# A transformer pair in one kernel: spill count read and Sqrt's table asked for before a stage barrier, second sum of squares of the first later layer taken from unscaled rows

## What is computed

```python
def rms_norm(x, w):
    xf = x.astype(jnp.float32)
    y = xf * lax.rsqrt(jnp.mean(xf * xf, axis=-1, keepdims=True) + NORM_EPS)
    return (y * w.astype(jnp.float32)).astype(x.dtype)
...
    return rms_norm(h, norm_final_w)          # end of the first block
...
    for l in range(DEPTH_2):
        h = rmsnorm(x, g_pre_mix[l])          # entry of a later layer
        y = token_mixer(h, w_in[l], ...)
        x = x + rmsnorm(y, g_post_mix[l])
        h = rmsnorm(x, g_pre_ffn[l])
        y = conv_ffn(h, w_up[l], ...)
        x = x + rmsnorm(y, g_post_ffn[l])
```

## Time and profile before

| what | value |
|---|---|
| median of 3 runs | 2921.39 us (2921.37 to 2924.36) |
| the profiled execution's own time | 2923.01 us |
| its span | 2921.1 us |
| mean granted TensorE clock, share of full | 0.97 |
| busy: PE, DVE, ACT, POOL | 2684.8, 1318.0, 873.6, 707.5 us |
| last unite on DVE | 1676.02 to 1677.24 |
| first Square of the entry | 1680.52 |
| first transposes of layer 0 | 1686.72 |
| first product of layer 0 | 1689.55 |

### The profile page before, as it was taken

The page is one execution under the profiler, slowest core; times in us unless marked ns, Lnnn a source line. Parts: engine busy times, 40 slices in busy tenths (PEclk is TensorE's granted clock), DMA queues, the critical chain, the costliest instruction groups (busy, mean ns, idle before and its releaser), DMA issues.

```text
span 2921.1 us, 35506 instructions
## 1 busy us (share of the span) xinstructions
PE 2684.8 (92%) x14188; PEld 1915.6 (66%) x14188; DVE 1318.0 (45%) x2403; ACT 873.6 (30%) x1643; POOL 707.5 (24%) x310
## 2 busy tenths in 40 slices
PE   8999999999988888888888789999999999899998
PEld 7997877888533333333333277688888776788887
DVE  4333745314633333333333367454444574644433
ACT  3333333423111111111111143543332344433332
POOL 4232233442000000000000122234445122344443
PEclk9999999999999999999999989999999999999999
DMA  3222211335999999999999721022232221122231
GB/s 142 87 88 103 78 65 37 107 114 210 382 427 427 429 428 429 428 429 429 428 429 428 332 85 58 30 87 87 93 109 87 90 89 58 58 87 87 89 113 72
DMA packets 126801, 572.19 MB, mean 196 GB/s; under 512 B 10705, under 2 KB 58193, under 8 KB 101329
## 3 DMA queue, kind: packets, MB, share of 16 engines
q1 hardware_dynamic: 121424, 561.08, 48.2%
q10 hardware_dynamic: 5248, 9.32, 1.0%
HBM read 566.12 MB, written 4.26 MB: 195 GB/s over the span
## 4 chain that ended last, share of the span: by engine, by line
PE 63%; DMA 25%; DVE 6%; ACT 3%; issue 1%; POOL 1%; POOLq 0%; SPq 0%; ACTq 0%; DVEq 0%
PE ps L342 39%; DMA wide<-in_moe_w 17%; PE ps L1262 8%; DMA arena<-in_moe_w 6%; PE ps L1690 4%; PE ps L1674 3%; PE ps L567 2%; PE ps L1060 1%; PE ps L538 1%; ACT ring_r L299 1%; PE ps L553 1%; DMA ring<-in_w_in 1%; DMA ring<-in_w_up 1%; PE ps L2604 1%; PE ps L2612 1%
## 5 line engine op out<-in xcount | busy, mean ns | idle before, releaser
L311 POOL TENSOR_TENSOR ring_r<-ring,ring_r 128x1024 fp32r<-128x1024 f32 (+2 forms) x284 | 692.5, 2471 | 2134.9 <-ACT ring_r L299 2134.9
L342 PE MATMUL ps<-xnT_r,ring_r 128*128 128x512 f32 (+1 forms) x1664 | 490.9, 378 | 9.9 <-DVE xn_r L2574 8.5
L342 PE MATMUL ps<-ring_r,xnT_r 128*128 128x512 f32 (+1 forms) x1360 | 446.3, 400 | 10.5 <-POOLq L255 5.0
L342 PEld LDWEIGHTS ps<-xnT_r,ring_r 128*128 128x128 f32 x1664 | 308.8, 191 | 69.8 <-DVE xn_r L2574 9.3
L342 PE MATMUL ps<-ring_r,arena_r 128*128 128x512 f32 x1392 | 329.9, 395 | 0.0
L342 PEld LDWEIGHTS ps<-ring_r,xnT_r 128*128 128x128 f32 x1360 | 290.0, 225 | 55.9 <-issue 11.6
L342 PE MATMUL ps<-xn_r,ring_r 128*128 128x512 f32 (+1 forms) x832 | 313.0, 376 | 0.0
L342 PEld LDWEIGHTS ps<-ring_r,arena_r 128*128 128x128 f32 x1392 | 262.3, 190 | 60.2 <-issue 5.4
L299 ACT ACTIVATE ring_r<-ring 128x1024 fp32r<-128x1024 f32 (+2 forms) x284 | 270.6, 1024 | 88.6 <-DMA ring<-in_w_down 68.3
L1674 PE MATMUL ps<-wide,arena 128*32 128x512 f32 x1536 | 199.3, 641 | 101.6 <-DMA wide<-in_moe_w 101.1
L1674 PEld LDWEIGHTS ps<-wide,arena 128*32 128x32 f32 x1536 | 42.0, 112 | 238.6 <-DMA wide<-in_moe_w 144.8
(11 more groups left out here) (358 smaller groups left out, 3681.1 us busy)
## 6 DMA issues: line engine op xcount, KB each, us to landing
wide<-in_moe_w SPq DMA_DIRECT2D x144, 2048.0 KB, 27.6
arena<-in_moe_w SPq DMA_DIRECT2D x48, 2048.0 KB, 27.4
ring<-in_w_in SPq DMA_DIRECT2D x25, 2048.0 KB, 8.1
ring<-in_w_up SPq DMA_DIRECT2D x22, 2048.0 KB, 8.5
ring<-in_w_down SPq DMA_DIRECT2D x10, 2048.0 KB, 7.8
ring<-in_w_out SPq DMA_DIRECT2D x6, 2048.0 KB, 8.1
ring<-in_w_ret_branch SPq DMA_DIRECT2D x2, 2048.0 KB, 8.7
attn_spill<-arena ACTq DMA_DIRECT2D x2, 1056.0 KB, 6.8
```

Source lines behind the costliest of these rows:

```text
L311: nc.gpsimd.tensor_tensor(ring_r[:, q % 2, cols], ring[:, q % 2, cols], ring_r[:, 2 + q % 2, cols].bitcast(F32), ALU.subtract).then_inc(ha ...
L342: ins = nc.tensor.matmul(bank, left, right, start=(start and k == 0), stop=(stop and k == 2))
```

## The change

Four things are changed, and only for the entry of the first later layer (`current["l"] == 0`) and the spill stage ahead of it.

The number of spills is read by `spill_count` ahead of the barrier on PE, DVE and ACT and handed to the spill functions; SP reads it where it did. ACT's small Sqrt for layer 0 stands between that read and the barrier, no longer at the entry.

DVE writes `xn` = `h` * `rows[:, 3]` for all four tiles (`gains_ready`). The branch of tile i then is the reciprocal, with `tile_added` on it, and h = xn * rstd, a tensor_scalar. Branches 0 and 1 stand in the loop behind products 0 and 1, products 2 and 3 behind them, and following 0 behind the loop.

Root h on ACT takes the Square of `xn` with rstd as its scale, and waits only for the reciprocal. The order of the roots in layer 0 becomes y0, h0, y1, h1, then behind the copies of tile 0 y2 and h2, behind those of tile 1 y3, behind those of tile 2 h3.

```diff
-        def spills(eng, body):
-            n = eng.value_load(spill_info[0:1, SPILL:SPILL + 1], min_val=0, max_val=SPILL)
+        def spill_count(eng):
+            return eng.value_load(spill_info[0:1, SPILL:SPILL + 1], min_val=0, max_val=SPILL)
+
+        def spills(eng, body, n):
             with eng.If(n > 0):
...
-                    for root in ((("h", 1), ("y", 3)), (("h", 2),), (("h", 3),), ())[k]:
+                    for root in enter_roots()[(4, 6, 7, 8)[k]:(6, 7, 8, 8)[k]]:
                         enter_root_act(a, *root)
...
+        FIRST_ENTER_ROOTS = [(what, i) for i in range(NT) for what in ("y", "h")]
         ENTER_ROOTS = [("y", 0), ("y", 1), ("h", 0), ("y", 2), ("h", 1), ("y", 3), ("h", 2), ("h", 3)]
...
-            if what == "h":
+            scale = 1.0
+            if what == "h" and current["l"] == 0:
+                a.wait_ge(Z.tile_added, i + 1)
+                x, scale = xn[:, i, :], small[:, BRANCH + 8 + i:BRANCH + 9 + i]
+            elif what == "h":
                 a.wait_ge(Z.tile_added, i + 1)
                 x = h[:, i, :]
...
-            nc.scalar.activation(Y.enter_squares[:, n % 2], x, ACT.Square, accum_out=small[:, base + i:base + i + 1]).then_inc(Z.sums_ready, 1)
+            nc.scalar.activation(Y.enter_squares[:, n % 2], x, ACT.Square, scale=scale, accum_out=small[:, base + i:base + i + 1]).then_inc(Z.sums_ready, 1)
...
             if current["l"]:
                 high_act(a, 0)
-            nc.scalar.activation(small[:, 30:31], table("eps"), ACT.Sqrt)
-            enter_root_act(a, "y", 0)
-            enter_root_act(a, "y", 1)
-            enter_root_act(a, "h", 0)
-            enter_root_act(a, "y", 2)
+                nc.scalar.activation(small[:, 30:31], table("eps"), ACT.Sqrt)
+            for root in enter_roots()[0:4]:
+                enter_root_act(a, *root)
...
-            link(nc.vector.reciprocal(rstd, small[:, BRANCH + 4 + i:BRANCH + 5 + i]))
+            ins = nc.vector.reciprocal(rstd, small[:, BRANCH + 4 + i:BRANCH + 5 + i])
             if current["l"] == 0:
-                nc.vector.scalar_tensor_tensor(out=h[:, i, :], in0=h[:, i, :], scalar=rstd, in1=rows[:, 3], op0=ALU.mult, op1=ALU.mult).then_inc(Z.tile_added, 1)
+                ins.then_inc(Z.tile_added, 1)
+                v.wait_ge(Z.tile_added, i + 1)
+                nc.vector.tensor_scalar(h[:, i, :], xn[:, i, :], rstd, None, ALU.mult).then_inc(Z.rows_normed, 1)
...
+                if current["l"] == 0:
+                    v.wait_ge(Z.rows_normed, i + 1)
                 rstd = small[:, NEXT + 8 + i:NEXT + 9 + i]
...
-            enter_branch_dve(v, link, 0)
-            enter_branch_dve(v, link, 1)
+            if current["l"] == 0:
+                for i in range(NT):
+                    nc.vector.tensor_tensor(xn[:, i, :], h[:, i, :], rows[:, 3], ALU.mult).then_inc(Z.gains_ready, 1)
+                    if i < 2:
+                        v.wait_ge(Z.gains_ready, i + 1)
+                        enter_branch_dve(v, link, i)
+                v.wait_ge(Z.gains_ready, NT)
+            else:
+                enter_branch_dve(v, link, 0)
+                enter_branch_dve(v, link, 1)
             v.wait_ge(pre_row_loaded, current["l"] * 16 + 16)
             following(0)
...
             experts_act(a)
+            spilled_n = spill_count(a)
+            nc.scalar.activation(small[:, 30:31], table("eps"), ACT.Sqrt)
             nxt()
-            spill_act(a)
+            spill_act(a, spilled_n)
```

More of the change, by code:

```diff
@@ L1936, in body, with spill_pe @@
                 sp.sem_inc(spill_next, 1)
-            spills(sp, body)
-        def spill_pe(pe):
+            spills(sp, body, spill_count(sp))
+        def spill_pe(pe, spilled_n):
             def body(j):
@@ L1964, in body, with spill_dve @@
                 pe.drain().then_inc(spill_used, 1)
-            spills(pe, body)
-        def spill_dve(v):
+            spills(pe, body, spilled_n)
+        def spill_dve(v, spilled_n):
             nc.vector.tensor_scalar(E.ahead, E.slot, -float(CAP * EXPERTS), None, ALU.add).then_inc(Z.shifted, 1)
@@ L1996, in body, with spill_act @@
                     unite_dve(i).then_inc(Z.tile_united, 1)
-            spills(v, body)
+            spills(v, body, spilled_n)
             v.drain().then_inc(Z.spills_united, 1)
-        def spill_act(a):
+        def spill_act(a, spilled_n):
             def body(j):
@@ L2009, in body @@
                 keep_y_act(0).then_inc(Z.y_act, 1)
-            spills(a, body)
+            spills(a, body, spilled_n)
         U_LAYERS = U_EXPERTS
@@ L2952, in down_banks, with enter_roots @@
             return ps[:, 2 * i:2 * i + 2, :].rearrange("p b n -> p (b n)")
+        def enter_roots():
+            return FIRST_ENTER_ROOTS if current["l"] == 0 else ENTER_ROOTS
         def enter_root_act(a, what, i, last=False):
             base = BRANCH if what == "y" else NEXT
-            n = i if last else ENTER_ROOTS.index((what, i))
-            if what == "h":
+            n = i if last else enter_roots().index((what, i))
+            scale = 1.0
[3 more added lines that the diff above has]
+            elif what == "h":
                 a.wait_ge(Z.tile_added, i + 1)
@@ L2987, in enter_branch_dve @@
         def enter_branch_dve(v, link, i, last=False):
-            v.wait_ge(Z.roots_ready, (i if last else ENTER_ROOTS.index(("y", i))) + 1)
+            v.wait_ge(Z.roots_ready, (i if last else enter_roots().index(("y", i))) + 1)
             rstd = small[:, BRANCH + 8 + i:BRANCH + 9 + i]
-            link(nc.vector.reciprocal(rstd, small[:, BRANCH + 4 + i:BRANCH + 5 + i]))
+            ins = nc.vector.reciprocal(rstd, small[:, BRANCH + 4 + i:BRANCH + 5 + i])
             if current["l"] == 0:
-                nc.vector.scalar_tensor_tensor(out=h[:, i, :], in0=h[:, i, :], scalar=rstd, in1=rows[:, 3], op0=ALU.mult, op1=ALU.mult).then_inc(Z.tile_added, 1)
+                ins.then_inc(Z.tile_added, 1)
+                v.wait_ge(Z.tile_added, i + 1)
+                nc.vector.tensor_scalar(h[:, i, :], xn[:, i, :], rstd, None, ALU.mult).then_inc(Z.rows_normed, 1)
             else:
+                link(ins)
                 term = Y.enter_term[:, i % 2]
@@ L2999, in following @@
             def following(i):
-                v.wait_ge(Z.roots_ready, ENTER_ROOTS.index(("h", i)) + 1)
+                v.wait_ge(Z.roots_ready, enter_roots().index(("h", i)) + 1)
+                if current["l"] == 0:
+                    v.wait_ge(Z.rows_normed, i + 1)
                 rstd = small[:, NEXT + 8 + i:NEXT + 9 + i]
@@ L3089, in _ @@
             experts_pe(pe)
+            spilled_n = spill_count(pe)
             nxt()
-            spill_pe(pe)
+            spill_pe(pe, spilled_n)
             for l in range(LAYERS):
@@ L3116, in _ @@
             experts_dve(v, link)
+            spilled_n = spill_count(v)
             nxt()
-            spill_dve(v)
+            spill_dve(v, spilled_n)
             for l in range(LAYERS):
```

## The result

The change makes the kernel slower: 2928.53 us (median of 17 runs, 2925.43 to 2933.9) against 2921.48 us for the kernel before (17 runs, 2915.67 to 2927.08), ratio 1.0023, 95% interval 1.0016 to 1.003. The forecast was 2929.1 us and slower. The medians differ by 7.05 us; the interval of the ratio is 4.7 to 8.8 us.

The account below looks back on a forecast made before the run. The prediction took PE (63%) and the experts' weight DMA (25%) to bound the kernel. Delays of 2.8, 2.9 and 1.9 us made 7.7, added to the median 2921.39 for 2929.1 us; range 2926.0 to 2932.5.

Parts of the forecast that it names:

- The early count: Barrier before the spill stage: count read (0.49 us) hidden ahead of it; first Square at best 2.0 us sooner.
- The table load: Behind the spill branch on ACT: one Sqrt table load returns in the middle of root y0, costing 1.30 us.
- The sum: Layer 0 entry: 2.8 to tile 0's transposes, 2.9 and 1.9 for new waits, 7.7 us later in all.
- the rival of 0.28: Behind the spill branch: loads before both Square and Sqrt, Square 1.1 us later, 8.8 in all, 2930.2 us; chance 0.28.
- one of the prediction's own signs of being wrong: Behind the spill branch: a table load missing or doubled would show the prediction wrong.
- DVE's work ahead of tile 0: Before tile 0's norm: tensor_scalar 0.75 us, product 0 hidden, products 2 and 3 uncovered; transposes 2.8 us later overall.
- The waits at tile 0 and tile 1: DVE's low halves queue behind roots y2 and y3, now after ACT's copies: 2.9 and 1.9 us later.
- Not slower, by waits taken up later: PE's later waits in this stage absorb up to 2.1 us: 5.6 us later, 2927.0 us; chance 0.08.
- a smaller shift at the next barrier: Sign of being wrong: the shift at the second barrier is smaller than at job 1.
- The drain of a table switch: ACT's table load: the skill page adds some 1.38 us, giving 2.66 for 1.30; prediction followed the trace without it.
- The clock: TensorE around the entry gap: no second fall to 1.2 GHz; chance timing of its rise plus or minus 1.0 us.

Follow-up runs that it names:

- the run with the kept table: The changed kernel plus one small Sqrt at the end of ACT's skipped spill body; ratio 1.0013 to the kernel before.
- y2 ahead of the copies: The changed kernel with ACT taking root y2 before its copies of tile 0's transposes in layer 0; 2926.72 us, ratio 1.0016 to the kernel before.

## Why the prediction was right

**The early count: right.** The read is hidden, on DVE too, and gives 0.8 us (0.78 at the transposes with nothing else changed).

**The table load: the direction right, the size one load short.** The sum took one load in the middle of root y0, at a chance of 0.40. Two came, the rival of 0.28 and one of the prediction's own signs of being wrong: the Square 1.1 us later (3.61 for 2.48), the load ahead of Sqrt as in the earlier trace rows. The term was 1.30; the run with the kept table, which has its first reciprocal at 4.04 where the change has 6.47, puts it at 2.43. The rival's place for the first reciprocal is 6.45, and it stands at 6.47. The reason that it gave, a table unknown where the two ways meet, is not shown beside a walk by lines.

**DVE's work ahead of tile 0: right.** The tensor_scalar takes 0.75 us as worked out, product 0 is hidden, products 2 and 3 are not. With two loads the transposes should have come 3.9 us later and came 3.80 later. Not in the sum was the Square with a scale column: 1.15 against 1.05, so 0.10 and not at most 0.06; the earlier trace rows was DVE's price, not ACT's. The Trainium skill (ScalarE: Activation LUTs, What ACT_TABLE_LOAD costs) gives 93 ns for a pointer operand, which agrees.

**The waits at tile 0 and tile 1: right**, 2.77 us for 2.9 and 1.76 for 1.9; each was forecast some 0.15 too long, most of it because tensor_scalar and low half overlap (1694.10 + 0.75 against a start at 1694.77).

**The sum.** At equal clock the profile gives 8.3 us where the sum with two loads has 8.8, and the sum as forecast 7.7. At job 1 the profiles differ by 7.0: 7.7 and the missing load's 1.1, less 0.4 for small terms a little too large, less 1.3 for the clock. That the point forecast of 2929.1 lies within 0.6 us of the median is thus luck, a load too few against the clock's 1.3; the medians' interval, 4.7 to 8.8, holds all these sums.

**Not slower, by waits taken up later: in part.** The sum took nothing for it and the rival at most 2.1 us, and a smaller shift at the next barrier was named as a sign of being wrong. It is smaller, by 0.9 us, and the wait for ACT of the earlier trace rows is gone. That is too little to turn the result.

**The drain of a table switch.** By the Trainium skill (ScalarE: Activation LUTs, What ACT_TABLE_LOAD costs), with 1.38 us of drain to the one load of the sum, the sum would have been 9.1. The trace shows Sqrt at 1681.47 behind a load that ends at 1681.45, and one load removed gave 1.2 us, not 2.66: no drain of that size here. The section on table sets of the same page has a load before every activation that needs one. The trace agrees as far as every Sqrt had its table; it can't show whether the first Square needed the load that stands ahead of it.

**The clock: the fall right, the size not.** The gap was longer and brought no second fall, and the pause before job 1 didn't make it fall either (a grant of 1.00 from 1701.50 to 1707.40). But 5.9 against 3.1 us at 1.2 GHz was worth 1.29 us, more than the 1.0 that was allowed. That this was chance isn't shown: the changed kernel spends 3.63 us of its time at the low level waiting for the first product, before 0.85, and with that wait removed (y2 ahead of the copies) the 5.9 us came back.

## What to carry to other kernels

A function-table load asked for ahead of a branch was worth nothing here, and cost 1.2 us more than asking behind it, because the branch's body uses another table: end the body with the table wanted behind it, even if the body never runs. When an order list of one engine is changed, walk the other engine's queue with it; a wait for a root holds everything queued behind it, whether or not that needs the root. Extra work to shorten a chain was worth doing here for the first tile only, since the others had time. And a saving ahead of the first products is to be read behind them as well, as part of it can go into products at half clock.

## What the runs showed of the hardware

A register read behind a running DVE instruction overlapped it (0.22 us at 1676.00, with the unite running until 1676.62). A 128x1024 fp32 tensor_scalar with a scalar column takes 0.75 us on DVE where the tensor_tensor of the same size takes 1.22. The granted clock was 1.00 in the 2.4 us behind PE's last unite and 0.50 under tile 0's transposes; in the changed kernel it rose 3.1 us behind the first product, after a wait of 3.63 us; with the first product 2.8 us sooner it rose 5.9 us behind it.
